# Two token blocks of an encoder layer in another order: both MLPs last, x1 through DRAM

## What is computed

```python
mod = silu(c) @ w_ada + b_ada             # shift1, scale1, gate1, shift2, scale2, gate2
h = layernorm(x) * (1 + scale1) + shift1
z = h @ w_in + b_in                       # a_val, a_gate, b_gb, b_gc, b_x, g_a, g_b
u = a_val * sigmoid(a_gate)
u = silu(layernorm(causal_conv31(u) + conv_a_b, ln_a_g, ln_a_b))
y_a = u @ w_a_out + b_a_out
y_b = (b_gb * causal_conv3(b_gc * b_x)) @ w_b_out
out = (sigmoid(g_a) * y_a + sigmoid(g_b) * y_b) @ w_o + b_o
x = layernorm(alpha * x + (1 + gate1) * out, ln1_g, ln1_b)
h = layernorm(x) * (1 + scale2) + shift2
f = square(relu(h @ w_up + b_up))
x = layernorm(alpha * x + (1 + gate2) * (f @ w_down + b_down), ln2_g, ln2_b)
```

## Time and profile before

| | |
|---|---|
| median of 3 runs | 1412.69 us (1409.1 to 1413.34) |
| the profiled execution's own time | 1412.28 us |
| its span on the slowest core | 1411.2 us (cores from 1385.6) |
| busy: PE, DVE, ACT, POOL | 1225.5, 646.6, 425.4, 260.0 us |
| mean granted TensorE clock, cores | 0.933 to 0.946 |
| DMA | 130.5 MB, mean 92 GB/s |

### The profile page before, as it was taken

The page is one execution under the profiler, slowest core; times in us unless marked ns, Lnnn a source line. Parts: engine busy times, 40 slices in busy tenths (PEclk is TensorE's granted clock), DMA queues, the critical chain, the costliest instruction groups (busy, mean ns, idle before and its releaser), DMA issues.

```text
span 1411.2 us, 19086 instructions; the slowest of 8 cores (1385.6 to 1411.2 us)
## 1 busy us (share of the span) xinstructions
PE 1225.5 (87%) x6556; PEld 618.5 (44%) x6556; DVE 646.6 (46%) x997; ACT 425.4 (30%) x760; POOL 260.0 (18%) x130
## 2 busy tenths in 40 slices
PE   2489787847999779999997799997999779999996
PEld 1256455523444334444443366653444334444442
DVE  4544363352234484245238325555234584245227
ACT  2232132222212167431028423334211167431000
POOL 1201000010202200026650000000102200026640
PEclk8589899977999899999999799998999899999998
DMA  9946817592553613755545754356553613755422
GB/s 182 213 76 103 117 18 103 82 204 44 78 72 60 140 40 60 100 81 102 81 90 146 141 97 69 61 70 140 73 77 60 145 35 60 102 77 78 72 31 120
DMA packets 146524, 130.50 MB, mean 92 GB/s; under 512 B 20910, under 2 KB 139950, under 8 KB 146300
## 3 DMA queue, kind: packets, MB, share of 16 engines
q0 software_dynamic: 104144, 88.74, 43.3%
q1 hardware_dynamic: 42284, 40.52, 10.4%
HBM read 196.88 MB, written 8.39 MB: 145 GB/s over the span
## 4 chain that ended last, share of the span: by engine, by line
PE 69%; DVE 10%; DMA 10%; ACT 5%; issue 4%; SPq 1%; DVEq 0%; POOL 0%; ACTq 0%; POOLq 0%
PE bank L153 68%; DMA wb<-w_in 3%; DMA wb<-w_ada 3%; DVE wt L775 2%; DMA xt<-xs 2%; DMA nb<-cbuf 1%; SPq L130 1%; DMA arow<-rows 1%; DVE st L523 1%; ACT h2T L580 1%; ACT csq L797 1%; DVE st L994 1%; ACT hT L580 1%; DVE cbuf L792 1%; DVE x L1005 1%
## 5 line engine op out<-in xcount | busy, mean ns | idle before, releaser
L153 PE MATMUL bank<-hT,wb 128*128 128x396 bf16 (+2 forms) x2304 | 434.1, 343 | 34.5 <-DMA wb<-w_in 14.5
L153 PEld LDWEIGHTS bank<-hT,wb 128*128 128x128 bf16 x2304 | 228.1, 99 | 216.9 <-issue 58.6
L153 PE MATMUL bank<-h2T,wb 128*128 128x512 bf16 x1024 | 225.3, 382 | 4.9 <-DVE x L1005 4.9
L153 PE MATMUL bank<-wb,fT 128*128 128x512 bf16 x1024 | 227.2, 379 | 0.0
L1047 DVE TENSOR_TENSOR fT<-rr 128x512 bf16<-128x512 bf16 x128 | 103.8, 817 | 130.6 <-ACT rr L1045 130.1
L153 PEld LDWEIGHTS bank<-h2T,wb 128*128 128x128 bf16 x1024 | 100.6, 99 | 126.8 <-issue 9.2
L153 PEld LDWEIGHTS bank<-wb,fT 128*128 128x128 bf16 x1024 | 99.9, 98 | 119.5
L130 POOL DMA_DIRECT2D wb<-w_in x36 | 31.7, 881 | 601.1 <-PE bank L153 585.6
L388 POOL TENSOR_TENSOR wb<-wb,g2b 128x4096 bf16<-128x4096 bf16 x16 | 128.0, 8007 | 0.3
L1045 ACT ACTIVATE rr<-bank,pvec 128x512 bf16<-128x512 f32 x128 | 85.3, 687 | 111.2 <-PE bank L153 88.0
L528 ACT ACTIVATE sd<-mv,eps 128x1 f32<-128x1 f32 (+1 forms) x66 | 18.6, 293 | 257.5 <-DVE mv L525 205.2
(11 more groups left out here) (104 smaller groups left out, 1157.2 us busy)
## 6 DMA issues: line engine op xcount, KB each, us to landing
wb<-w_in POOLq DMA_DIRECT2D x20, 1024.0 KB, 14.9
xt<-xs SPq DMA_DIRECT2D x32, 512.0 KB, 5.0
wb<-w_up POOLq DMA_DIRECT2D x16, 1024.0 KB, 10.7
wb<-w_down POOLq DMA_DIRECT2D x16, 1024.0 KB, 8.7
wb<-w_ada POOLq DMA_DIRECT2D x12, 1024.0 KB, 20.5
nb<-cbuf SPq DMA_DIRECT2D x64, 128.0 KB, 5.4
wb<-w_in POOLq DMA_DIRECT2D x16, 512.0 KB, 7.5
y<-x SPq DMA_DIRECT2D x16, 512.0 KB, 2.7
```

Of the source, the lines that this page charges most:

```text
L153: inst = pe.h.matmul(out, lhsT, rhs, start=self.first, stop=last)
```

## The change

Blocks are no longer taken one after the other. The order on PE becomes: adaLN tiles 0 to 3; token mixing of block 0 up to merge, with LN0 of block 1 between its merge items; token mixing of block 1, with output projection, LN1 and second LN0 of block 0 between its GLU pairs; `up` of block 0, with the same stages of block 1 between its groups; `down` of block 0; `up` and `down` of block 1.

Around this:

- LN0 of block 0: four tiles before the adaLN tiles, five (`p1_front`) each behind one of the first five GLU pairs; `modulate` by chunk, the first before GLU.
- w_ada tiles leave the list and get buffers of their own (`ada_load`): 0 to 3 issued first, 4 to 7 after the second GLU pair, 8 and 9 at the start of p, 10 and 11 after these are used. 4 to 7 are used together after GLU, 8 and 9 together after p, 10 and 11 before merge.
- Weight slots are taken from a list of free ones instead of in turn.
- x1 goes to a DRAM tensor `x1d` and is loaded again before `down`.
- The residual x is added by DVE instead of by an fp32 matmul; LN1 reads it from SBUF.
- The convolution's LayerNorm starts within p (pair 17 on: statistics, then steps), one step per item; the diagonals of conv3 (`dg3`) are built per channel tile on DVE in place of once on POOL; `bc` holds LN1's rows, then LN2's.
- merge takes the B items of two channel tiles, then the A items.
- w_o of block 0 has buffers of its own, and both halves are scaled at the start of merge.

```diff
+    def ws_pump():
+        while ws["issued"] < len(wtiles) and ws["free"]:
+            i = ws["issued"]
+            s = ws["free"].pop(0)
...
+        def proj(t):
+            k = t % nx1
+            for h in range(2):
+                bi = brot.next()
+                grp = PEGroup(pe, bank_res[bi])
+                grp.mm(bank_ap[bi], e0, brow[:, h * 512:(h + 1) * 512], [r_const, r_rows])
+                for kc in range(KC):
+                    grp.mm(bank_ap[bi], mg[:, kc, t * 128:(t + 1) * 128], wo[h][0][:, kc, :],
+                           [r_mg[kc][t // 4], wo[h][1]], last=(kc == KC - 1))
+                hs = slice(h * 512, (h + 1) * 512)
+                dve.op(lambda e: e.tensor_tensor(x1[k][:, hs], bank_ap[bi], xt[t % nxt][:, hs], ALU.add),
+                       reads=[bank_res[bi], r_xt[t % nxt]], writes=[r_x1[k]])
+            ln_stats_a(x1[k], 128, slA[t % 4], r_x1[k])
+            ln_sqrt(128, slA[t % 4], eps2_t)
+
+        def ln1(t):
+            k = t % nx1
+            ln_recip(128, slA[t % 4], nmr=False)
+            ln_affine_dve(x1[k], 128, slA[t % 4], r_x1[k], bc[:, 0:1024], bc[:, 1024:2048])
+            ln_stats_a(x1[k], 128, slB[t % 4], r_x1[k])
+            ln_sqrt(128, slB[t % 4], eps_t)
+            sp.dma(drows(x1d, b, t), x1[k], own("x1s%d" % (t % nx1)), reads=[r_x1[k]], writes=[r_x1d[b][t]])
...
+    def p1_front(i):
+        P1["stats"](i)
+        P1["norm"](i)
+        P1["trans"](i)
+
+    for i in range(4):
+        p1_front(i)
+    for nt in range(4):
+        ada_tile(nt)
+    ada_finish()
...
+    modulate(0)
...
+        if b == 0:
+            for nt in (4, 5, 6, 7):
+                ada_tile(nt)
+            ada_finish()
...
+                    if nq < 16:
+                        conv_chunk(nq)
+                        nq += 1
+                    elif nn == 0 and "r" not in L:
+                        lna_stats()
+                    else:
+                        norm_step(nn)
+                        nn += 1
...
+        if b == 0:
+            ada_rows((OFF_TMP + 6144, OFF_WT + 8192))
+            ada_fetch(8)
+            ada_fetch(9)
+            ada_tile(8)
+            ada_tile(9)
+            ada_finish()
+            ada_fetch(10)
+            ada_fetch(11)
+            for i_, nt in enumerate((10, 11)):
+                ada_load(nt, OFF_H[1] + i_ * 8192, "h%d" % i_)
...
+    def glu0_side(n):
+        if n < 5:
+            if n == 0:
+                for i in range(4, 8):
+                    P1["load"](i)
+            p1_front(4 + n)
+            if n == 0:
+                P1["load"](8)
+        if n == 2:
+            modulate(1)
+        if n == 4:
+            modulate(2)
+        if n == 1:
+            ada_rows([OFF_TMP + 8192 + i_ * 2048 for i_ in range(4)])
+            for i_, nt in enumerate((4, 5, 6, 7)):
+                ada_load(nt, OFF_CB + i_ * 8192, i_)
...
+    def after_gb0():
+        ada_tile(10)
+        ada_tile(11)
+        ada_finish()
...
+        for h in range(2):
+            scale_tile(wo[h][0], wo[h][1], "g1", h)
...
+    def merge0_side(n):
+        if n >= 2 and n % 2 == 0 and state["p1s"]:
+            state["p1s"].pop(0)()
...
+    def glu1_side(n):
+        if n % 2 == 1 and p3s:
+            p3s.pop(0)()
...
+    def up0_side(n):
+        if n % 4 == 0 and p3s1:
+            p3s1.pop(0)()
+            if len(p3s1) == 2:
+                for w_ in wo1:
+                    ws_release(w_[2])
+
+    fT, r_fT = up(0, H2[0][0], H2[0][1], up0_side)
+    assert not p3s1
+    sp.dma(bc, bc_d[:, 2048:4096], own("bc"), writes=[r_bc])
+    down(0, fT, r_fT)
+    fT, r_fT = up(1, H2[1][0], H2[1][1], lambda n: None)
+    down(1, fT, r_fT)
```

More of the change, by code:

```diff
@@ L281, in newres, with own, grp4 @@
         return fw.new_res(name, off, off + nbytes)
+    owners = {}
+    def own(key):
+        if key not in owners:
+            owners[key] = Owner("%s" % key)
+        return owners[key]
+    def grp4(ap):
+        return ap.rearrange("p (r n) -> p r n", r=4)
     o = 0
@@ L343, in wfull @@
         wtiles.append([(0, 512, wsrc(w, r0, c0))])
-    def wsrc2(w, c0):
-        return w.rearrange("(kc p) c -> p kc c", p=128)[:, :, c0:c0 + 256]
-    for nt in range(4):
-        wfull(w_ada, 0, nt * 512)
     for b in range(NB):
-        ada = iter(range(4, 12) if b == 0 else ())
-        def wada(n):
-            for _ in range(n):
-                nt = next(ada, None)
-                if nt is not None:
-                    wfull(w_ada, 0, nt * 512)
         for g in range(2):
@@ L455, in build_program, with ada_load @@
     brot = Rot(range(6))
+    pst_rot = Rot((6, 7))
+    out_events = []
     SH1, SC1, SH2, SC2 = 0, 8, 16, 24
-    r_mod1, r_mod2 = Res("mod1"), Res("mod2")
-    ada = {"pend": None, "rows": None, "rot": None}
-    def ada_rows(off, n):
-        ada["rows"] = [(sb(off + i * 2048, [1, 512], F32, "arow"), newres("arow%d" % i, off + i * 2048, 2048)) for i in range(n)]
+    ada = {"pend": None, "side": {}}
+    def ada_load(nt, off, key):
+        t = sb(off, [128, 8, 512], BF16, "wada")
+        r = newres("wada%d" % nt, off, 8192)
+        dma_group(pool, [(t, wsrc(w_ada, 0, nt * 512))], own("ada%s" % key), writes=[r])
+        ada["side"][nt] = (t, r)
+        return r
@@ L463, in ada_rows @@
+    def ada_rows(offs):
+        n = len(offs)
+        ada["rows"] = [(sb(o_, [1, 512], F32, "arow"), newres("arow%d" % i, o_, 2048), own("arow%d" % i)) for i, o_ in enumerate(offs)]
         ada["rot"] = Rot(range(n))
+    ada["got"] = {}
     def ada_fetch(nt):
-        k = ada["rot"].next()
-        row, rr = ada["rows"][k]
-        sp.dma(row, rows_d[0:1, nt * 512:(nt + 1) * 512], rr, writes=[rr])
-        return row, rr
+        row, rr, ow = ada["rows"][ada["rot"].next()]
+        sp.dma(row, rows_d[0:1, nt * 512:(nt + 1) * 512], ow, writes=[rr])
+        ada["got"][nt] = (row, rr)
@@ L496, in ada_tile @@
     def ada_tile(nt):
-        row, rr = ada_fetch(nt)
-        wt, wr, wi = ws_get()
+        if nt not in ada["got"]:
+            ada_fetch(nt)
+        row, rr = ada["got"][nt]
+        wt, wr = ada["side"][nt]
         bi = brot.next()
@@ new lines, in pipeline, with run, xrows, drows @@
+    def pipeline(stages, n):
+        steps = []
+        for step in range(n + len(stages) - 1):
+            def run(step=step):
+                for sidx in reversed(range(len(stages))):
+                    i = step - sidx
+                    if 0 <= i < n:
+                        stages[sidx](i)
+            steps.append(run)
+        return steps
+    def xrows(b, t):
+        return xs[HALO + b * TB:HALO + (b + 1) * TB].rearrange("(n r) d -> r n d", r=R)[t]
+    def drows(a, b, t):
+        return a[b * TB:(b + 1) * TB].rearrange("(n r) d -> r n d", r=R)[t]
@@ L643, in p1_setup @@
-        steps = []
-        for step in range(nti + len(stages) - 1):
-            def run(step=step):
-                for sidx in reversed(range(len(stages))):
-                    i = step - sidx
-                    if 0 <= i < nti:
-                        stages[sidx](i)
-            steps.append(run)
-        return dict(hT=hT, r_hT=r_hT, tiles=tiles), steps
-    ctx, steps = p1_setup(0, raw=True)
-    ada_rows(OFF_WT, 4)
-    nada = 0
-    for k_, st_ in enumerate(steps):
-        st_()
-        if k_ >= 3 and nada < 4:
-            ada_tile(nada)
-            nada += 1
```

765 lines of the change are left out of this document (343 added, 422 removed).

## The result

The changed kernel took 1436.52 us, median of 4 runs (1433.17 to 1471.77), beside 1413.01 for the kernel before on the same chip: a ratio of 1.0171 (95% interval 1.0142 to 1.0200). The forecast was 1344, with 1288 to 1400. It was wrong in sign and by 93 us.

What follows compares the result with a forecast made beforehand. The prediction took TensorE as the bound, busy 1225.5 of 1411.2 us, with losses in idle time and low clock. Stage times summed to 1333, plus 10 for the clock's return and 1.1 around the span: 1344, range 1288 to 1400.

Steps and rivals of the forecast that it cites:

- wait for the row: Between p and v of block 0: adaLN rows of tiles 8 and 9 fetched behind 24 nb issues, waiting from 268 to 297.
- clock's return: Whole span: 10 us added for the clock to return after some ten waits.
- The fronts: Block 0's GLU: five LN0 tiles between pairs, each leaving PE 6.2 us idle plus 0.9 of transposes, 36 us in all.
- The step of GLU 1: Block 1's GLU with block 0's LN1 between pairs: 13.3 us a step on DVE against PE's 9.2.
- the sign of "wrong altogether": No wait at 268 to 297, or any wait for x1 or a weight tile, would show the forecast wholly wrong.
- v1 at 40 us: v stage of block 1: 40 us against 51 before, as nb transfers have seven pairs more to land in.
- down 0 at 112.5 and up 1 at 109.3: MLP stages: down of block 0 takes 112.5 us, up of block 1 109.3, with nothing added for reloading x1.
- merge 0's coupling, 11: Block 0's merge with block 1's LN0: nine steps of 8.0 or 9.8 us on DVE against PE's 7.4 lose 11.
- B: Overlapped stages: six banks let PE run ahead, so DVE's waits vanish; 1292 us, chance 0.25.
- C: Overlapped steps: the table load before the root is exposed too, 23 x 1.28 = 29 us, to 1373; chance 0.13.
- D: Fronts, merge 0, GLU 1, up 0: PE's gaps lower the clock; at 0.68 it gives 1433; chance 0.08.
- E: PE-bound stages: denser TensorE on all cores lowers the clock from 1.00 to 0.89, 120 us more, 1465; chance 0.04.

Runs made afterwards that it cites:

- run 7: Changed kernel with silu steps later, block 0 GLU's LN0 transposes a pair later, adaLN rows fetched early, next w_down scaling flushed between down's halves: ratio 0.9847.
- the six edits: Changed kernel with silu later, LN0 transposes later, adaLN rows early, w_down scaling flushed between down's halves, roots later, x1 reload later: median 1324.16 us, ratio 0.9388.

## Why the prediction was wrong

The sum ahead was 1343; the profile has 1436. By its own terms, with the borders from PE's timeline:

| step of the forecast | forecast | measured | difference |
|---|---|---|---|
| GLU 0 ends | 163 | 165 | +2 |
| adaLN 4 to 7 | 20 | 27 | +7 |
| p0 | 85 | 97 | +12 |
| wait for the row | 29 | 40 | +11 |
| v0, adaLN 10 and 11 | 47 | 47 | 0 |
| merge 0 | 127 | 138.5 | +11.5 |
| GLU 1 | 120 | 128 | +8 |
| p1 | 86 | 89 | +3 |
| v1 | 40 | 54 | +14 |
| merge 1, up 0 | 268 | 271 | +3 |
| down 0 | 112.5 | 130 | +17.5 |
| up 1 | 109.3 | 124 | +14.7 |
| down 1 and tail | 126 | 127 | +1 |
| clock's return | 10 | in the rows above | -10 |

The borders of up 0 and down 0 are those of the windows above, where POOL issues the next tile. Five steps make most of the 93 us: down 0 and up 1 (32), v1 (14), p0 (12), merge 0 (11.5) and the row (11); what each had wrong is said below.

**Right.** The fronts: gaps of 5.9 us (forecast 6.2), the stage to within 2 us. The step of GLU 1: 13.2 (13.3), the waits of PE there 27.4 us (excess 28); the rest of the difference is PE's own busy time, 97.9 instead of 92, at a clock of 0.96. This one is right in its mechanism as well: the forecast had 10.9 us of DVE's own work and 2.4 of root, load and sigmoid, the trace has waits of 2.38, and with the roots later the step is 10.6. Down 1 and tail are within 1 us, and the wait for the row is at the place named. Up 0 is within 1 us too, but in part by luck: PE waits 8.7 us for the LN1 steps where the forecast had 13, and 3.3 us of the wait at the border to down 0 make up for it. Of the signs named ahead, DVE over 80% busy in GLU 1 failed (9.5 of 13.2 us in a step, 72%: the waits are its own), and the sign of "wrong altogether", a wait for a weight tile, came.

**Wrong 1: v1 at 40 us, "the nb transfers have seven pairs more to land in".** That counts only when a transfer lands. What decides is who is in line behind its reader. In v the silu stands on ScalarE ahead of the sigmoids, and one late nb (10.5, then 6.9 us) stops ACT, DVE and PE in turn. Moving the silu alone gave 24 us in the two blocks; moving the whole LayerNorm back gave 17, nearly all of it in v0. The forecast had asked what is queued behind a wait on SP, and not on ScalarE.

**Wrong 2: down 0 at 112.5 and up 1 at 109.3, "a row of x1 is needed 40 us after its reload is issued: nothing".** The row of x1 indeed cost nothing. In up 1 the 4 MB of it, with 4 MB of y, delayed others: w_up tiles at 38.0 us to landing, 9.6 us of waits, which the late reload takes away. It is the question that the forecast answered for the reader and not for the neighbours in the DMA engines. A mean share of 0.4 to 0.6 over a stage said nothing about 50 us in which it is 0.95 to 1.10 (1185 to 1240 us). Down 0 has nothing from the reload. It waits 6.2 us for an unscaled tile, which the flush of run 7 takes away, and 3.9 us of the 7.2 behind the stalled squares (the other 3.3 lie in the window of up 0). The forecast saw squares of up to 8.8 us and argued that PE never stopped after them; it did not stop because many groups of up lay behind, and at the border to down there are none. That POOL's scaling is the cause of these long squares is read from their times alone and was not tested. The clock adds the rest: at 0.95 and 0.96 in these windows the work takes 119.8 and 114.5 us instead of 112.5 and 109.3. In the median of the cores the two stages take 122.5 and 116.5 us, so some 15 of the 32 us are the slowest core's own.

**Wrong 3: merge 0's coupling, 11.** It is 21.4 us of waits. The forecast set 8.0 or 9.8 us a step against PE's 7.4, with 2.4 us in which DVE waits for root, one table load and sigmoid. Those 2.4 hold only where DVE has other work during the load before the root, as in GLU 1. In merge 0 it has none, both loads are in its wait, and that is 3.76. Add the 1.36 us to the forecast's own steps: 9.4 and 11.2 against 9.35 to 11.08 measured, and 8 x 1.36 = 11 us more, about the difference in the table. The roots-later run takes all 21.4 away with the same work on DVE, so it is a round trip and not DVE's load: DVE's aggregate, ACT's load and root, ACT's load and sigmoid behind it, DVE's product. More than half of PE's waits, 11.6 us, are for xn at the transposes, where a free bank is of no help.

**Wrong 4: small terms, all on one side.** adaLN 4 to 7 is 7 over (clock 0.66, DMA share 1.09 in its window), p0 12 over (PE busy 88.9 us and idle 8.2, against 84.7 and 4.3 for the same work in p1; why was not tested), and so the nb issues begin 22 us later than assumed. The row's wait is 11 longer in itself: the 24 issues take 27.8 us and not 23, and the row lands 12 us after its group's first issue where the forecast had left 5. The reserve of 10 us for the clock's return was one for all places.

**The rivals.** B, that six banks absorb DVE's waits (1292), is excluded: they don't, though most waits are only 1 to 3 us. C, both loads of a step exposed (1373), is right in merge 0, with the reason that it gave, that DVE has little else to do there, and wrong in seven of nine steps of GLU 1; it is 11 us of the 93 by which the forecast was off. That removing the loads gains 46 us doesn't make them the only cure: keeping all of them and issuing the root later gains 42, since no sigmoid then stands behind a root that waits. D, a low clock, was to be seen by less than 0.75 in merge 0, GLU 1 and up 0; they have 1.00, 0.96 and 0.99. E, less than 1.00 in a gapless stage, doesn't hold: 785 to 896.5 us has PE busy for all 111.50 us at 1.00. The rule of the Trainium skill (TensorE: Matmul & The Clock Gate, Seeing it yourself, where it stands), 1.95 GHz once three cores of a die run dense matmuls, would show as 0.81 here and isn't borne out by this profile: from 800 to 890 us all eight cores have 1.00.

The other page weighed, the Trainium skill (ScalarE: Activation LUTs, What ACT_TABLE_LOAD costs), gives 2.66 us a switch, a drain included. Here a load is 1.28 us in all 56 places, the next instruction follows within 0.02, and where ScalarE goes from a root straight to the next load, that begins within 0.02 as well: no drain shows. The timeline has 32 loads in waits that end on PE's path (5 in the fronts, 16 in merge 0, 11 in GLU 1), 41 us at 1.28, where the run without them gains 46. The forecast had counted 23. The run with later roots shows that most of this is the price of the place, not of the load.

The order of the stages itself isn't what cost the time: with the six edits the same order gives 1324. The gains that the runs took back lie in the order within the engines' queues: ScalarE (roots, silu), SP (rows behind nb), POOL (scaling asked for late), the DMA engines (reload beside weights). I had 0.10 on slower, all of it on the clock; none of my cases was "several queues at once, each for 10 to 25 us", and a range to 1400 held no room for it.
